# Projections of h as seven block products a pair, with X in DRAM meanwhile, and interleaved first FFN output groups

## What is computed

```
h = rms_norm(x, g_pre_mix) * (1 + sc1) + sh1
mq, mk, mv, mo, mi, mf, su, sv, wq, wk, wv, gl = split_in(h @ p['w_in'])
...   # A: mLSTM on mq, mk, mv, gated by mo; B: spatial gating on su, sv; C: attention on wq, wk, wv
gates = jax.nn.sigmoid(gl).reshape(B, S, N_BRANCH, D_MODEL)
merged = (gates[:, :, 0] * (y_ml @ p['w_br_mlstm'])
          + gates[:, :, 1] * (y_sg @ p['w_br_gmlp'])
          + gates[:, :, 2] * (y_sw @ p['w_br_swa']))
x = x + g1 * rms_norm(merged @ p['w_out'], p['g_post_mix'])
h2 = rms_norm(x, p['g_pre_ffn']) * (1 + sc2) + sh2
gate, up = jnp.split(h2 @ p['w_ffn_in'], 2, axis=-1)
f = (jax.nn.silu(gate) * up) @ p['w_ffn_out']
x = x + g2 * rms_norm(f, p['g_post_ffn'])
```

## Time and profile before

| | us |
|---|---|
| median of three runs | 2050.78 |
| the profiled execution | 2051.14 |
| its span in the profile | 2049.3 |
| TensorE busy (16121 matmuls) | 2017.6 |
| vector engine busy | 1105.2 |
| GpSimd busy | 1040.4 |
| ScalarE busy | 687.5 |

### The profile page before, as it was taken

How to read it: one execution, slowest core, us unless ns; L and a number is a source line. 1 busy time by engine, 2 the same in 40 slices (tenths; PEclk the granted TensorE clock), 3 DMA queues, 4 the chain that set the end, 5 groups by cost and what they waited for, 6 DMA issues and landing times.

```text
span 2049.3 us, 38703 instructions
## 1 busy us (share of the span) xinstructions
PE 2017.6 (98%) x16121; PEld 1944.4 (95%) x16121; DVE 1105.2 (54%) x1769; ACT 687.5 (34%) x1476; POOL 1040.4 (51%) x552
## 2 busy tenths in 40 slices
PE   8999999999999999999999999999999999999998
PEld 7998898999999999999999989889999999999997
DVE  5222466467647545647563245664765573647473
ACT  4111224123334342425532111341243343525253
POOL 0444454565673736354734544546648445354543
PEclk9999999999999999999999999999999999999999
DMA  9746222223351443323544342222234312232332
GB/s 362 260 138 63 56 80 58 69 72 94 94 189 37 137 127 88 89 79 102 175 141 146 62 63 82 58 59 75 72 93 136 122 52 83 83 93 84 92 94 77
DMA packets 300093, 211.94 MB, mean 103 GB/s; under 512 B 14048, under 2 KB 294160, under 8 KB 296720
## 3 DMA queue, kind: packets, MB, share of 16 engines
q1 hardware_dynamic: 293168, 205.94, 34.8%
q10 hardware_dynamic: 6752, 3.53, 0.7%
HBM read 204.65 MB, written 4.07 MB: 102 GB/s over the span
## 4 chain that ended last, share of the span: by engine, by line
PE 92%; DVE 2%; DMA 2%; POOL 2%; ACT 1%; issue 1%; SPq 0%; DVEq 0%; POOLq 0%; ACTq 0%
PE ps L1063 36%; PE ps L1155 20%; PE ps L1091 13%; PE ps L1782 5%; PE ps L1175 3%; PE ps L1181 2%; DMA raw<-in_w_in 2%; PE ps L1308 1%; PE ps L1223 1%; PE ps L1523 1%; PE ps L1687 1%; PE ps L1650 1%; PE ps L1538 1%; PE ps L1665 1%; PE ps L1202 1%
## 5 line engine op out<-in xcount | busy, mean ns | idle before, releaser
L1063 PE MATMUL ps<-h_hi,hi_lo 128*128 128x288 f32 x2560 | 464.4, 299 | 0.3 <-POOL hi_lo L962 0.3
L959 POOL TENSOR_TENSOR hi_lo<-raw,consts 128x1024 fp32r<-128x1024 f32 (+1 forms) x112 | 222.2, 1984 | 449.7 <-PE ps L1063 313.6
L1063 PEld LDWEIGHTS ps<-h_hi,hi_lo 128*128 128x128 f32 x2560 | 381.4, 190 | 8.2 <-issue 5.3
L990 POOL TENSOR_TENSOR a_lo<-raw,a_hi 128x512 fp32r<-128x512 f32 x108 | 159.9, 1481 | 270.6 <-ACT a_hi L2363 270.6
L962 POOL TENSOR_TENSOR hi_lo<-raw,hi_lo 128x1024 fp32r<-128x1024 f32 (+1 forms) x112 | 279.3, 2494 | 8.8
L1063 PE MATMUL ps<-h_lo,hi_lo 128*128 128x288 f32 x1280 | 274.7, 296 | 0.0
L1063 PEld LDWEIGHTS ps<-h_lo,hi_lo 128*128 128x128 f32 x1280 | 207.1, 189 | 0.0
L1091 PE MATMUL ps<-yf_hi,fo_h 128*128 128x288 f32 x704 | 152.3, 298 | 2.9 <-DVE yf_lo L2538 2.9
L1091 PE MATMUL ps<-yf_hi,fo_l 128*128 128x288 f32 x704 | 150.7, 296 | 0.0
L1091 PE MATMUL ps<-yf_lo,fo_h 128*128 128x288 f32 x704 | 150.4, 295 | 0.0
L959 POOL TENSOR_TENSOR hx<-raw,consts 128x1024 fp32r<-128x1024 f32 x26 | 52.2, 2006 | 145.8 <-PE ps L1181 63.6
(11 more groups left out here) (450 smaller groups left out, 5102.2 us busy)
## 6 DMA issues: line engine op xcount, KB each, us to landing
ada<-in_w_ada SPq DMA_DIRECT2D x23, 2048.0 KB, 9.2
raw<-in_w_in SPq DMA_DIRECT2D x88, 512.0 KB, 3.8
raw<-in_w_ffn_in SPq DMA_DIRECT2D x144, 256.0 KB, 3.1
raw<-in_w_ffn_out SPq DMA_DIRECT2D x32, 384.0 KB, 3.4
raw<-in_w_in SPq DMA_DIRECT2D x40, 256.0 KB, 3.8
raw<-in_w_ffn_out SPq DMA_DIRECT2D x32, 320.0 KB, 3.1
raw<-in_w_out SPq DMA_DIRECT2D x16, 512.0 KB, 3.8
raw<-in_w_ffn_in SPq DMA_DIRECT2D x16, 512.0 KB, 4.8
```

The source lines that it names most:

```text
L959: pool.tensor_tensor(hi, RAW[s][:, 0:size], ONES[:, 0:1].to_broadcast([128, size]), ALU.mult).then_inc(chunk_hi, 1)
L990: pool.tensor_tensor(lo[:, :], RAWB[o], hi[:, :].bitcast(f32), ALU.subtract).then_inc(s_alo, 1)
L1063: m = pe.matmul(o[:, h, :], a[:, k, c0:c0 + 128], mv(k, h), start=(k == 0 and begins), stop=(k == nk - 1 and a is wl))
```

## The change

- The 20 plain groups v, mo, wq, su, sv of a layer become 10 pairs (HPAIRS) of seven products (`h_products`). They need T1 to T4 of h, made once a layer by eight vector operations on 1152 columns each (`h_whole`, `h_less`), four roundings on ScalarE (`ht_high`) and four low parts (`ht_low`). T1 and T2 take the place of X in SBUF, T3 and T4 the place of y.
- For that, X goes to a DRAM tensor `x_kept` by a DMA that ScalarE issues after it has copied qk1 (`spill_x`), and comes back by one on SP's queue among the loads of the first branch. The vector engine waits for the way out before it makes T1, and for the way back before the norm behind `wo`.
- The split weights of the pairs have four places that go round (`h_place`): the operand number i may be written once product i - 4 is done. The weight sums are made in SBUF, in the place of the low part (s2 in a place of its own).
- The results of products are accumulated in two PSUM units that are held for all ten pairs (`hc`, `hr`); all the small groups of this part take turns in the other two.
- The small groups are put between single products: scores, for example, in two parts between p6, p2 and p7. The attention slots start three slots later: sc0 stands in the last pair, slots 1 to 11 among the first branch's gates.
- The first gate chunk (P_BR) has its split weights in X's place too; y's rows, WIN and NM lie elsewhere.
- In FFN blocks 1 and 2 the output groups 0 and 1 are interleaved (`first_groups`): all k but the last of both, then the last k of both.

```diff
+HPAIRS = [(nm, n) for nm in ("v", "mo", "wq", "su", "sv") for n in (0, 2)]
+MIX = ["hc", "hr", "gt3", "kt0", "vt0", "vt1", "cm0", "kt1", "cm1", "vt2", "kt2", "cm2", "vt3", "kt3", "cm3"]
...
+for _h in range(4):
+    MIX += _a(_h)[:1] + (_b(_h - 1)[1] if _h else []) + _a(_h)[1:] + _b(_h)[0]
+MIX += _b(3)[1] + ["r4", "r0", "r1", "ko", "r2", "r3", "svt0", "svt1", "sc0"]
...
+        def h_place(q, o):
+            i = (7 * q + H_OPERANDS.index(o) + 2) % 4
+            c = slice(i % 2 * WH, i % 2 * WH + WH)
+            return HILO[i // 2][:, 0, c], HILO[i // 2][:, 1, c], HLS[i // 2][:, 1, c]
...
+        def h_place_free(eng, l, q, o):
+            i = 7 * q + H_OPERANDS.index(o)
+            if i < 4:
+                eng.wait_ge(chunk_used, last_in(l, (1 - i // 2,)))
+            else:
+                eng.wait_ge(h_prod, l * (7 * NHP) + (i - 3))
...
 # SP
+                def h_blocks_read(o, n):
+                    if o != "a21":
+                        sp.wait_ge(h_alo, 3 * n + {"a11": 1, "a12": 2, "a22": 3}[o])
+                    sp.wait_ge(h_sum, 4 * n + {"a11": 3, "a21": 3, "a12": 4, "a22": 1}[o])
...
+                for q, (nm, n) in enumerate(HPAIRS):
+                    c = {"v": C_V, "mo": C_MO, "wq": C_WQ, "su": C_SU, "sv": C_SV}[nm] + n * 128
+                    for o in ("a11", "a21", "a12", "a22"):
+                        h_block(o, q, c)
...
+                        if (b, n) == (0, 4):
+                            sp.wait_ge(x_spilled, l * 16 + 16)
+                            sp.wait_ge(chunk_used, done(l, "g0_0"))
+                            sp.dma_start(X[:, :, :].rearrange("p k c -> p (k c)"), XD).then_inc(x_back, 16)
...
 # GpSimd
+                for q in range(NHP):
+                    for o in ("a11", "a12", "a22"):
+                        h_block_lo(o, q)
...
 # TensorE
+                def first_groups(c, nb, mh, ml, moving):
+                    out_group(c, 0, nb, mh, ml, moving, ks=range(nb - 1))
+                    group_begins(c, 1)
+                    out_group(c, 1, nb, mh, ml, ks=range(nb - 1))
+                    out_group(c, 0, nb, mh, ml, moving, ks=(nb - 1,))
+                    out_group(c, 1, nb, mh, ml, ks=(nb - 1,))
...
+                def h_products(q, *xs):
+                    for i, x in enumerate(xs):
+                        if i == 0:
+                            h_begins(q, x)
+                        wh, wl, _ = h_place(q, WEIGHTS[x])
+                        bh, bl = H_DATA[x]
+                        o = h_rest(l)[:, x != "p2", :] if x in ("p2", "p5", "p3") else h_chain(l, q)
+                        for k in range(4):
+                            for a, mv in ((wh, bh), (wh, bl), (wl, bh)):
+                                if k == 3 and a is wl and i + 1 < len(xs):
+                                    h_begins(q, xs[i + 1])
+                                m = pe.matmul(o, a[:, k * 128:(k + 1) * 128], mv(k), skip_group_check=True,
+                                              start=(k == 0 and mv is bh and a is wh and x in ("p1", "p5", "p2")),
+                                              stop=(k == 3 and a is wl))
+                        m.then_inc(h_prod, 1)
...
                 for h in range(4):
+                    row_spread(h)
+                    h_products(3 + h, "p1")
+                    if h:
+                        back(h - 1)
+                    h_products(3 + h, "p5", "p6")
+                    scores(h, 0)
+                    h_products(3 + h, "p2")
+                    scores(h, 1)
+                    h_products(3 + h, "p7")
+                    outputs(h)
+                    h_products(3 + h, "p3", "p4")
...
+                h_products(7, "p1")
                 back(3)
+                h_products(7, "p5")
                 rope(4)
+                h_products(7, "p6", "p2")
                 rope(0)
+                h_products(7, "p7", "p3")
                 rope(1)
+                key_window()
+                h_products(7, "p4")
+                h_products(8, "p1", "p5", "p6", "p2")
                 rope(2)
+                h_products(8, "p7", "p3", "p4")
...
 # ScalarE, before the first product and in a head
+                h_block_high("a11", 0)
+                h_sum_high(1, 0)
+                h_sum_high(2, 0)
                 modulation_tiles("wk")
                 tile("wk", KA[:, 0:T])
+                h_block_high("a12", 0)
...
+                for h in range(4):
+                    h_keep(0, 3 + h)
+                    decay(h)
+                    h_sum_high(3, 3 + h)
+                    after_p5(3 + h)
+                    if h:
+                        head_hi(h - 1)
+                    after_p6(3 + h)
+                    after_p2(3 + h)
...
+                    after_p7(3 + h)
+                    after_p3(3 + h)
+                    after_p4(3 + h)
...
 # vector engine
+                    if i == 4:
+                        h_whole(3, 0, 1)
+                        h_whole(4, 1, 0)
+                        dve.wait_ge(x_spilled, l * 16 + 16)
+                        h_whole(1, 0, 0)
+                        h_less(1, 3, 1, 3)
+                        h_whole(2, 1, 1)
+                        h_less(3, 2, 3, 5)
+                        h_less(2, 2, 1, 5)
+                        h_less(4, 4, 2, 7)
...
+                def after_p7(q):
+                    h_half(q)
+                    h_weights(1, q + 1)
+                    h_weights(2, q + 1)
+
+                def after_p3(q):
+                    h_first_tile(q)
+                    h_weights_low(1, q + 1)
...
                 for h in range(4):
+                    exponents(h)
+                    after_p1(3 + h)
...
+                    if h:
+                        gate_head(h - 1)
+                    after_p5(3 + h)
+                    weigh_scores(h)
+                    if h:
+                        y_lo(h - 1, YT[:, :])
+                    after_p6(3 + h)
+                    after_p7(3 + h)
                     normalise(h)
...
+                    after_p3(3 + h)
+                    after_p4(3 + h)
```

More of the change, by code:

```diff
@@ L224, in unit_turns @@
     first = G[1, f"fo{NB - 1}_0"]
-    ring, others = first % UNITS, 0
+    ring, at, others = list(range(UNITS)), 0, 0
     for i, (l, n) in enumerate(ORDER):
[L227 to L230, removed]
+        if n == "hc":
+            held = [ring[(at + x) % len(ring)] for x in range(UNITS)]
+            ring, at = held[2:], 0
+            u = held[0]
+        elif n == "hr":
+            u = held[1]
+        else:
+            if n == "g0_0":
+                ring, at = [held[1], ring[at % 2], ring[(at + 1) % 2], held[0]], 0
+            if l == 1 and i >= first:
+                u = ring[(at + 3) % UNITS] if n[:2] == "gk" else ring[(at + others % 3) % UNITS]
+                others += n[:2] != "gk"
+            else:
+                u = ring[at % len(ring)]
+                at += 1
         unit[l, n], turn[l, n] = u, turns[u]
@@ L286, in slots @@
 def slots():
-    last, out, prior = {0: -2, 1: -1}, {}, {}
+    last, out, prior = {0: -2, 1: -1, 5: None}, {}, {}
     for l in range(DEPTH):
@@ L480, in weights @@
                 pair = HI[s], LO[s]
+            elif s == 5:
+                pair = X5
             elif l == 1 and pos <= 4 and s > 2:
@@ L1592, in _, with row_columns @@
[L1592 to L1601 removed]
+                def row_columns():
+                    pe.wait_ge(unit_of(l, "gt3"), empty(l, "gt3"))
+                    pe.wait_ge(rows_ready, nth(rows_ready, l))
+                    pe.wait_ge(tables_loaded, 16 if l == 0 else 48)
+                    o = unit(l, "gt3")
+                    for x, c in ((AR, 0), (WR, 20), (EM, 44)):
+                        for t in range(NTT + 1):
+                            n = 128 if t < NTT else 64
+                            pe.transpose(o[0:n, c + 4 * t:c + 4 * t + 4], x[:, t * 128:t * 128 + n], IDN[0:4, 0:4])
+                    for h in range(4):
+                        m = pe.matmul(o[:, 40 + h:41 + h], SEL[0:4, h, :], WIN[:, 63:64], start=True, stop=True)
+                    m.then_inc(done_by("gt3"), 1)
@@ new lines, in after_p1, with after_p5, after_p6, after_p2 @@
+                def after_p1(q):
+                    h_keep(0, q)
+                    h_sum_high(3, q)
+                def after_p5(q):
+                    h_keep(1, q)
+                    h_sum_high(4, q)
+                def after_p6(q):
+                    h_keep(2, q)
+                    h_block_high("a22", q)
+                def after_p2(q):
+                    h_block_high("a11", q + 1)
+                def after_p7(q):
+                    h_sum_high(1, q + 1)
+                    if HPAIRS[q][0] == "mo":
+                        h_tanh(q, False)
@@ L2059, in _ @@
                        .then_inc(c_stored, 16)
-                for h in range(4):
-                    if h >= 2:
-                        act.wait_ge(done_by(f"vt{h - 2}"), done(l, f"vt{h - 2}"))
```

(1 more changed line is left out.)

623 lines of the change are left out of this document (441 added, 182 removed).

## The result

The changed kernel took 2056.11 us, median of 20 runs (2050.68 to 2066.05), against 2050.78 (2048.28 to 2054.81) in 20 runs of the kernel before: a ratio of 1.0025, 95% interval 1.0017 to 1.0034, so a little slower. The forecast was 2023, in a range of 2016 to 2034. The profiled execution took 2051.73 us, at the quick end of its 20.

What follows compares the result with a forecast made beforehand. It took the sum of TensorE's instructions as the bound (busy 2017.6 of 2049.3 us). Terms -32.4 - 2.9 + 2 + 3 + 1 + 1.5 = -27.8 (1.5 for pair 0's start and the end) took 2050.8 to 2023, range 2016 to 2034.

Steps and rivals of the forecast that it cites:

- The loop through block a22: Projection pairs: reloading and splitting a22 in the ring of four places delays p5 of the next pair; +3 heads, +1 others.
- Busy time down by 31 to 33: Sign expected in the profile: TensorE's busy time falls by 31 to 33 us.
- Idle time up by at most 6: Sign expected in the profile: TensorE's idle time, 31.7 us before, rises by at most 6 us.
- The spill: X out to DRAM and back in each layer, some 10.3 us a transfer: hidden, bounds 0 to 4 us, taken as 0.
- Rival C: Layer 0: spill or start stalls, qk5's load late by all of 10 us, +5 to +6: 2029; chance 0.15.
- The projections: Ten pairs in each layer: 84 matmuls for 96 save 1.62 us a pair, 32.4 us less TensorE work.
- +2 for returns: Small fp32 groups between products: 38 more returns to projection matmuls, 0 to 0.2 us each, taken at 0.05.
- The vector engine: Projection pairs: 6.7 us more work each, 14.7 of 18.6 us in a head, up to 18.0 with holds; no bound.
- D: Rival: the vector engine becomes the bound in heads and pairs 7 to 9, +63 for +4: 2082; chance 0.03.
- B: Rival: the a22 loop decides in most pairs, 1 us or more in each of 20: 2039; chance 0.13.
- E: Rival: pairs run but each product's first matmul pays a return, 28 us in all: 2051; chance 0.03.
- Interleaving: FFN blocks 1 and 2, both layers: interleaved output groups cover four waits for low parts, -2.9 us, bounds -2.9 and 0.

Runs made afterwards that it cites:

- run 3: Changed kernel with the vector engine's copy of v(3) and weighting of keys(3) put ahead of pair 3's two weight sums: 2057.5 us.
- run 9: Changed kernel with the n columns turned by a TensorE transposition and stored as rows of 512 bytes, all outputs written: 2030.33 us, 0.9901 of the kernel before.
- run 11: Changed kernel with n stored as 512-byte rows, and the FFN output groups of blocks 1 and 2 in order again: 2033.97 us.
- run 10: Changed kernel with n stored as 512-byte rows, and only 64 KB of X spilled in layer 0 (outputs of no use): 2024.62 us, 0.9876 of the kernel before.
- Run 12: Changed kernel with n stored as 512-byte rows, and X's spill issued behind qk3's copy, 7.7 us later: 2026.92 us, 0.9883 of the kernel before.
- run 5: Changed kernel with the n columns copied to their own tile and stored late, as two transfers ahead of the last plain FFN chunk: 2037.32 us.
- run 8: The kernel before without its stores of n (outputs n not written): 2050.82 us, 0.9997 of the kernel before.
- run 2: Changed kernel without the eight stores of n in each layer (outputs n not written): 2030.18 us, 0.9899 of the kernel before.

## Why the prediction was wrong

**The step that failed** is in "The loop through block a22": "the next a22 lands after 3.1". I took the landing of a block from the FFN's median in the earlier trace rows for every pair. In pair 3 it is 11.0 and 10.6 us, since ScalarE's state stores run then. The loop has a margin of 1 to 2 us, not 8. What then waited wasn't p5, as the loop had it, but state(3), whose keys stood behind the late sum in the vector engine's order; run 3 shows that p5 would have been next, 3.35 us late. I had no term for either, nor for the clock. The two stops and their clock are 24.4 us, of the 33 between forecast and result. Taking the 4-byte rows away gave 25.8 by medians (run 9). Between the profiled executions it gave 21.7 (2049.6 to 2027.9), with pair 0 starting 2.5 us later in run 9 (125.44 against 122.93), which nearly makes up the difference. I had counted the DMAs that the change issues, and not those already there that its new loads would meet. The row that warned was in the trace of before: 512 KB landed in 16.8 us at just that place. A median over 88 loads hid it.

**The signs named.** 240 matmuls fewer: 224 fewer are recorded. Busy time down by 31 to 33: 20.9, and 26.4 in run 9 (1991.2), since matmuls at the lower clock count longer and, as worked out below, returns cost more than I took. Idle time up by at most 6: it rose by 21.2. No wait of output groups in blocks 1 and 2: so it is. One of 0.9 stands at block 3, which had none before; it is there in run 11 too, so it isn't the interleaving's.

**Five other steps.**
- The spill, "hidden, barely; I take 0": wrong, and above its upper bound of 4. qk5's split starts at 64.83 us in place of 58.63, 6.2 late against the 5 I worked out, and TensorE waits there, 2.1 to 5.0 us in every run of the changed kernel but 10 and 12. With the later start of pair 0 it costs 5.7 us (10 against 9). The transfer took 12.1 us in layer 0 and 14.4 in layer 1, not 10.3. Rival C had the mechanism and the cost, +5 to +6, as one case of 0.15, though with a load 10 us late, not 6.2. The Trainium skill says that transfers of all issuing engines interleave on the same 16 DMA engines (DMA: Bandwidth & Descriptors, Issuing engines are not separate DMA queues). The row at 64.83 agrees, and run 10 by 5.7 us. Run 12's 3.4 us point the same way, but its interval and that of run 9, on another chip, overlap.
- The clock had no term. A stop of 7.8 us brought 5.2 more at the 1.2 GHz level, one of 7.3 us 4.1 more.
- The projections: -32.4 with +2 for returns, +3 and +1 for the loop: -26.4 where nothing stalls. Run 9 has -27. The sum is right and its parts aren't, so its fit is in part luck. No product waits in the heads, yet a head takes 19.4, not 18.6: groups of 12 take 1.79 behind small work and 1.58 elsewhere, so a return is the upper 0.2, not 0.05. 38 of them are 7.6. The gross gain must then be nearer the 34 of the other price, 2 x 6.43 - 11.14 = 1.72 a pair, 34.4: -34.4 + 7.6 = -26.8.
- The vector engine: its share rose by 7 points, as forecast. Sums take 0.69 to 0.76 and low parts 0.68 in the heads of run 9, so GpSimd, with three low parts of 1.32 us in 19.4, hardly holds them. The engine is busy 13.8 of 19.4 us in a head (55.3 us in four), far from D. No product waited over 1 us in every pair (B), and run 9 shows no sign of E.
- Interleaving: -2.9 forecast, -3.6 by medians (11), its four waits gone as said.

Without the stops and the spill the time comes out at the forecast: run 10 has 2024.6 against 2023. That is close partly because errors cancel, as the projections show. The range of 2016 to 2034 was a fair one for the steps that I had listed; it held nothing for a cause that I hadn't.

## What to carry to other kernels

When a change cuts a fetch-ahead of whole chunks to one of blocks, look up every transfer of the stage, stores too, and read the landing times stage by stage rather than by median: slack that the old prefetch had may be hiding them. Stores of a column as 4-byte rows cost nothing visible where they are issued; what they delay is the next load. Turn them into rows with a transposition, which won back all of it here; putting them in a stretch without loads won back only part (run 5). Whether a deeper fetch-ahead of blocks would have hidden them too wasn't tried. And when TensorE stops for some us, add to the stop what the clock takes after it.

## What the runs showed of the hardware

- Four stores of 128 rows of 4 bytes (2 KB in all) delayed the landing of a 256 KB load on another queue to 11 us, or 15 to 18 with nothing between them, against 3.0 without. The DMA engines moved 33 to 38 GB/s meanwhile in layer 0. In layer 1 they moved 1 GB/s for 5 us, and the load counted as landed 7.6 us after its last bytes had started to move. In the kernel before, two loads of 512 KB landed in 16.8 us with such stores and in 3.7 without (run 8).
- Without the 16 stores of n the page counts 12448 packets under 512 bytes in place of 14752 (run 2), 144 fewer for each store of 128 values. The Trainium skill says that below 512 bytes a transfer makes a DMA engine read, modify and write (DMA: Bandwidth & Descriptors, Specifications), and that a last dimension that isn't contiguous becomes one descriptor for each element and is best rearranged (Rules for kernel authors). The packets agree with the second, at least one for each value, and so does run 9, by 26 us. The first may be why the stores hold up loads; no run separates it from the count of rows.
- In run 5 TensorE stopped for 4.0 and 3.2 us, 10 to 12 us behind such stores, with no weight or result late by the profile.
- In a stop of 7.8 us the granted clock fell to 0.50, the 1.2 GHz level, and stayed there for 11 us more in which TensorE worked; after one of 4.0 us (run 5) it was 0.72 over the ten us behind.
